# A third K-tile pair by seven products in the up projections, and the retention output from split factors

## The reference

```python
def swiglu(x, w_up, w_down):                      # FFN_HIDDEN = 5632, called twice
    g, u = jnp.split(x @ w_up, 2, axis=-1)
    return (jax.nn.silu(g) * u) @ w_down

def retention(q, k, v):                           # 4 heads, key width 256, value width 512, chunk 128
    ...
        inner = jnp.einsum('bhid,bhjd->bhij', qi, ki) * intra
        o = jnp.einsum('bhij,bhjv->bhiv', inner, vi) + jnp.einsum('bhid,bhdv->bhiv', qi * q_decay, state)
    ...

h = h + 0.5 * rms_norm(swiglu(rms_norm(h, ffn1_pre), ffn1_up, ffn1_down), ffn1_post)
h = h + rms_norm(hybrid_mixer(rms_norm(h, mix_pre), ...), mix_post)
h = h + 0.5 * rms_norm(swiglu(rms_norm(h, ffn2_pre), ffn2_up, ffn2_down), ffn2_post)
```

## Time and profile before

| | |
|---|---|
| median of 3 runs | 2403.52 us |
| the profiled execution: its time | 2403.92 us |
| its span in the trace | 2402.1 us |
| granted TensorE clock, mean | 0.999 |
| PE busy | 2386.3 us, 99%, 10711 instructions |
| PEld busy | 1963.1 us, 82% |
| DVE busy | 1556.8 us, 65%, 1789 instructions |
| ACT busy | 1170.9 us, 49% |
| DMA | 470.98 MB, mean 196 GB/s |

### The profile page before, as it was taken

How to read it: one execution, slowest core, us unless ns; L and a number is a source line. 1 busy time by engine, 2 the same in 40 slices (tenths; PEclk the granted TensorE clock), 3 DMA queues, 4 the chain that set the end, 5 groups by cost and what they waited for, 6 DMA issues and landing times.

```text
span 2402.1 us, 34068 instructions
## 1 busy us (share of the span) xinstructions
PE 2386.3 (99%) x10711; PEld 1963.1 (82%) x10711; DVE 1556.8 (65%) x1789; ACT 1170.9 (49%) x1400; POOL 201.1 (8%) x392
## 2 busy tenths in 40 slices
PE   9999999999999999999999999999999999999998
PEld 7888888888887888887888888888788888888887
DVE  5888888874456555655545545555788888886444
ACT  5555545554445454444534444444655555555443
POOL 1212112110000000000000000000021212111000
PEclk9999999999999999999999999999999999999999
DMA  7665666665656455564666565655566666666564
GB/s 238 211 212 196 226 205 210 218 220 180 205 175 194 152 183 171 162 189 156 200 191 194 192 196 191 194 177 184 176 216 216 210 214 195 226 207 219 191 195 156
DMA packets 265730, 470.98 MB, mean 196 GB/s; under 512 B 21056, under 2 KB 54512, under 8 KB 265296
## 3 DMA queue, kind: packets, MB, share of 16 engines
q1 hardware_dynamic: 252752, 453.04, 58.2%
q0 software_dynamic: 12752, 17.24, 2.3%
q10 hardware_dynamic: 176, 0.07, 0.0%
HBM read 456.64 MB, written 2.10 MB: 191 GB/s over the span
## 4 chain that ended last, share of the span: by engine, by line
PE 98%; DVE 1%; issue 0%; DMA 0%; ACT 0%; POOL 0%; DVEq 0%; ACTq 0%; POOLq 0%
PE acc L673 25%; PE acc L674 24%; PE acc L675 24%; PE acc L766 6%; PE acc L765 6%; PE acc L764 6%; PE bank L764 2%; PE bank L765 2%; PE bank L766 2%; PE bank L694 1%; DVE h L1474 0%; DVE w_lo L1410 0%; PE bank L994 0%; DVE xT_lo L1421 0%; PE bank L934 0%; PE bank L960 0%
## 5 line engine op out<-in xcount | busy, mean ns | idle before, releaser
L1410 DVE TENSOR_TENSOR w_lo<-w_raw,w_hi 128x1024 fp32r<-128x1024 f32 x856 | 1023.9, 1199 | 728.2 <-ACT w_hi L1094 720.8
L1094 ACT ACTIVATE w_hi<-w_raw 128x1024 fp32r<-128x1024 f32 x856 | 888.6, 1040 | 1101.9 <-PE acc L675 845.6
L673 PE MATMUL acc<-w_hi,xT_hi 128*128 128x512 f32 x1664 | 655.3, 394 | 4.1 <-DVE xT_lo L1421 2.4
L675 PE MATMUL acc<-w_hi,xT_lo 128*128 128x512 f32 x1664 | 648.1, 389 | 0.0
L674 PE MATMUL acc<-w_lo,xT_hi 128*128 128x512 f32 x1664 | 647.8, 389 | 0.0
L673 PEld LDWEIGHTS acc<-w_hi,xT_hi 128*128 128x128 f32 x1664 | 312.5, 188 | 71.8 <-DVE xT_lo L1421 3.4
L675 PEld LDWEIGHTS acc<-w_hi,xT_lo 128*128 128x128 f32 x1664 | 312.4, 188 | 65.9
L674 PEld LDWEIGHTS acc<-w_lo,xT_hi 128*128 128x128 f32 x1664 | 312.6, 188 | 64.3 <-issue 1.0
L673 PE MATMUL acc<-w_hi,act_hi 128*128 128x512 f32 x704 | 273.9, 389 | 0.0
L675 PE MATMUL acc<-w_hi,act_lo 128*128 128x512 f32 x704 | 273.9, 389 | 0.0
L674 PE MATMUL acc<-w_lo,act_hi 128*128 128x512 f32 x704 | 273.9, 389 | 0.0
(11 more groups left out here) (202 smaller groups left out, 1862.0 us busy)
## 6 DMA issues: line engine op xcount, KB each, us to landing
w_raw<-in_ffn_up_dram SPq DMA_DIRECT2D x352, 512.0 KB, 4.1
w_raw<-in_ffn_down_dram SPq DMA_DIRECT2D x176, 512.0 KB, 4.1
w_raw<-in_w_gate_dram SPq DMA_DIRECT2D x96, 512.0 KB, 3.7
w_raw<-in_w_in_dram SPq DMA_DIRECT2D x72, 512.0 KB, 3.5
w_raw<-in_w_in_dram SPq DMA_DIRECT2D x128, 256.0 KB, 3.0
w_raw<-in_w_ret_out_dram SPq DMA_DIRECT2D x32, 512.0 KB, 4.7
w_raw<-in_w_out_dram SPq DMA_DIRECT2D x32, 512.0 KB, 4.4
act_raw<-blocks POOLq DMA_DIRECT2D x352, 32.0 KB, 3.7
```

The costliest lines, as they stand in the source:

```text
L673: pe.matmul(pair[m][:, :], xh, wh, start=(first and kk == 0), stop=False)
L675: mm = pe.matmul(pair[m][:, :], xl, wh, start=False, stop=(last and kk == KG - 1))
L1094: act.activation(w_hi[:, s, cols], w_raw[:, s, cols], ACT.Copy).then_inc(w_rounded, 1)
L1410: dve.tensor_tensor(w_lo[:, s, cols], w_raw[:, s, cols], w_hi[:, s, cols].bitcast(f32), ALU.subtract).then_inc(w_split, 1)
```

## The change

`QUADS` has a third pair, so in each of the 20 up strips three K-tile pairs are multiplied by seven products; the order of the groups moves; the third quad uses the first one's place for its sums again. The gate's second token tile is finished before, not behind, the group that DVE splits next. In the heads loop the retention output is made by three fp32r matmuls for each product: ACT and DVE split `innerT` and the value strip into hi and lo parts.

```diff
-QUADS = ((4, 5, 6), (10, 11, 7))
-PLAIN_GATE = ((0, 0), (1, 1), (2, 2), (3, 3), (6, 4), (7, 5))
-PLAIN_UP = ((8, 0), (9, 1), (12, 2), (13, 3), (14, 4), (15, 5))
+QUADS = ((5, 6, 5), (9, 10, 6), (12, 13, 7))
+PLAIN_GATE = ((0, 0), (1, 1), (2, 2), (3, 3), (4, 4))
+PLAIN_UP = ((7, 0), (8, 1), (11, 2), (14, 3), (15, 4))
...
-        T_SLOT = (0, 1)
+        T_SLOT = (1, 0, 1)
...  SP, at the end of an up strip's loads
+                    sp.wait_ge(t_summed, 3 * (quad(f, i, NQUAD - 1) + 1))
+                    sp.sem_inc(slot_summed, 1)
...  PE, heads, n == 25
+            def inner_values(b, block, m, start, stop):
+                cols = slice(block * P, (block + 1) * P)
+                pe.matmul(bank[b][:, :], inner_hi[:, cols], v_hi[:, m, :], start=start, stop=False)
+                pe.matmul(bank[b][:, :], inner_hi[:, cols], v_lo[:, m, :], start=False, stop=False)
+                return pe.matmul(bank[b][:, :], inner_lo[:, cols], v_hi[:, m, :], start=False, stop=stop)
...
+                        pe.wait_ge(inner_split, g + 1)
                         claim("o", 2, g)
-                        pe.matmul(bank[2][:, :], innerT[:, 0:P], gate_sb[:, 0, :], start=True, stop=True).then_inc(filled[2], 1)
+                        inner_values(2, 0, 0, True, True).then_inc(filled[2], 1)
                         claim("o", 3, g)
-                        pe.matmul(bank[3][:, :], innerT[:, P:2 * P], gate_sb[:, 0, :], start=True, stop=False)
-                        pe.matmul(bank[3][:, :], innerT[:, 2 * P:3 * P], gate_sb[:, 1, :], start=False, stop=True).then_inc(filled[3], 1)
+                        inner_values(3, 1, 0, True, False)
+                        inner_values(3, 2, 1, False, True).then_inc(filled[3], 1)
...  ACT, up strip
-                        if n == 10:
+                        if n == 12:
                             wait_filled(act, f"p{f}", 0, i)
                             act.activation(p1_sb[:, :], bank[0][:, :], ACT.Copy).then_inc(read[0], 1)
-                        if n == 13:
+                        if n == 15:
                             wait_strip_read(act, sec, i, 0)
...
-                                    wait_quad_used(act, f, NST - 1, NQUAD - 1)
+                                    wait_quad_used(act, f, NST - 1, 1)
                                 hidden_hi(f, n - 12)
...
+                wait_quad_used(act, f, NST - 1, NQUAD - 1)
                 with act.Fori(0, CH // 2) as i:
...  ACT, heads
+                    if n == 20:
+                        wait_read(act, "inner", 0, g)
+                        act.activation(inner_hi[:, :], innerT[:, :], ACT.Copy).then_inc(inner_rounded, 1)
                     if n == 23:
-                        strip_out(g, n, 2, ACT.Copy)
+                        wait_strip(act, "heads", g, n)
+                        act.wait_ge(rs_ready, MEAN["pre1"] + 1)
+                        for m in range(MT):
+                            last = act.activation(v_hi[:, m, :], acc[pair_of("heads", 2)][m][:, :], ACT.Copy,
+                                                  scale=rs_pre[:, 1, m:m + 1])
+                        last.then_inc(v_rounded, 1)
...  DVE, up strip
-                dve.wait_ge(t_used, quad(f, i, j) + 1)
+                dve.wait_ge(t_used, quad(f, i, j) + (2 if j == 0 else 1))
...
-                        if n == 11:
+                        if n == 13:
                             wait_quad_used(dve, f, i, NQUAD - 1)
...
                             dve.tensor_tensor(u3_sb[:, :], u2_sb[:, :], bank[3][:, :], ALU.add).then_inc(read[3], 1)
-                            wait_filled(dve, f"p{f}", 1, i)
-                            dve.tensor_tensor(u4_sb[:, :], u2_sb[:, :], bank[1][:, :], ALU.add).then_inc(combined, 1)
-                        if n == 12:
                             wait_read(dve, f"p{f}", 3, i)
                             dve.scalar_tensor_tensor(gate_sb[:, 1, :], u3_sb[:, :], to_tile1[:, 0:1], gate[1][:, :],
                                                      ALU.mult, ALU.add).then_inc(acc_read[pair_of(sec, 0)], 1)
+                        if n == 14:
+                            wait_filled(dve, f"p{f}", 1, i)
+                            dve.tensor_tensor(u4_sb[:, :], u2_sb[:, :], bank[1][:, :], ALU.add).then_inc(combined, 1)
                             dve.tensor_tensor(u5_sb[:, :], u3_sb[:, :], bank[1][:, :], ALU.add).then_inc(read[1], 1)
...  DVE, heads
+                    if n == 21:
+                        dve.wait_ge(inner_rounded, g + 1)
+                        dve.tensor_tensor(inner_lo[:, :], innerT[:, :], inner_hi[:, :].bitcast(f32), ALU.subtract).then_inc(inner_split, 1)
+                    if n == 23:
+                        dve.wait_ge(v_rounded, g + 1)
+                        for m in range(MT):
+                            last = dve.scalar_tensor_tensor(v_lo[:, m, :], acc[pair_of("heads", 2)][m][:, :], rs_pre[:, 1, m:m + 1],
+                                                            v_hi[:, m, :].bitcast(f32), ALU.mult, ALU.subtract)
+                        last.then_inc(acc_read[pair_of("heads", 2)], 1)
```

More of the change, by code:

```diff
@@ L169, in hybrid_trunk @@
         hid_sb = sb("hid_sb", [P, MT, STRIP], f32)
+        v_hi = sb("v_hi", [P, MT, STRIP], f32r, at=tmp_at)
+        v_lo = sb("v_lo", [P, MT, STRIP], f32r, at=tmp_at + 4 * MT * STRIP)
         junk = sb("junk", [P, D], f32, at=tmp_at)
@@ L247, in hybrid_trunk @@
         o_junk = sb("o_junk", [P, STRIP], f32, at=s_at)
+        q_at = place["at"]
         qT = sb("qT", [P, 2, SEQ], f32)
+        inner_hi = sb("inner_hi", [P, 3 * P], f32r, at=q_at)
         winT = sb("winT", [P, 2, SEQ], f32)
@@ L251, in hybrid_trunk @@
         rkT = sb("rkT", [P, 2, SEQ], f32)
+        inner_at = place["at"]
         innerT = sb("innerT", [P, 3 * P], f32)
+        inner_lo = sb("inner_lo", [P, 3 * P], f32r, at=inner_at)
         decay = sb("decay", [P, 2 * P], f32)
@@ L304, in hybrid_trunk @@
         k_now_ready = sem("k_now_ready")
+        v_rounded = sem("v_rounded")
+        inner_rounded = sem("inner_rounded")
+        inner_split = sem("inner_split")
         dve_step = sem("dve_step")
```

## The result

| | before | changed |
|---|---|---|
| median, four runs of each | 2403.52 us | 2388.89 us |
| lowest to highest | 2403.48 to 2403.59 | 2388.06 to 2389.58 |
| the profiled execution: time, span | 2403.92, 2402.1 us | 2389.05, 2387.2 us |

The ratio is 0.9939, 95% interval 0.9923 to 0.9955: 14.6 us less. Forecast were 2386.0 us and a range of 2384.3 to 2393.0. The median lies inside that range, but above the 2384.5 to 2388 that the forecast itself gave 0.62; it is in the stretch of rival 1.

A forecast was written before the change was run, and what follows sets the result against it. PE was taken to bound the kernel (98% of the chain). -13.6 - 2.1 - 2.2 + 0.4 = -17.5 from the profiled 2403.92 us gives 2386.4, and 2386.0 us for the median; range 2384.3 to 2393.

The forecast's parts named there:

- rival 1: Gain smaller: small wait moves elsewhere, fp32r beside transposes no faster, last strips lose up to 1 us each; 2387 to 2392, chance 0.16.
- The bound: Whole kernel: PE makes up 98% of the chain, so time goes only where PE does less or waits less.
- part 1: Third quad in each of 20 up strips: three matmuls fewer a strip, 60 x 0.2267 us, -13.6 us.
- The wait for `t_lo`: Up strips: PE's 18 waits for the last `t_lo` of a quad go, 0.12 us each, -2.1 us.
- DVE's dates: Up strips: DVE, 94% busy, still finishes each operand before PE wants it; cost 0.
- The room behind the third quad: Up strips: the third quad's second `t_lo` ends at T = 32.8, 1.9 us before PE needs it.
- The last strip: Last up strip of each block, with two hidden tiles more on DVE: cost 0, up to 1 us in each of two blocks.
- Part 3: Heads loop, retention output: nine fp32r steps (2.04 us) for six float32 records (2.58), four heads, -2.2 us.
- Part 4: Token sums: two more transposes for each block, 4 x 0.11 us, +0.4 us.
- The sum: Whole kernel: all terms together, -17.5 us against the profiled execution's 2403.92 us.
- rival 2: Up strips: loads between quads come late and PE stalls; with 1.6 us late each, 2412 us; chance 0.10.
- rival 3: Up strips: DVE a little behind, each strip loses 0.3 to 0.5 us; 2392 to 2397 us, chance 0.12.

The follow-up runs named there:

- e3: The kernel before, still two quads, with only the first quad one group later (groups 5 and 6 in place of 4 and 5): 2402.11 us.
- e6: The changed kernel with the split of group 14 made twice in each up strip, one DVE instruction more: 2389.24 us.
- e7: The changed kernel with the split of group 14 made three times in each up strip, two DVE instructions more: 2407.05 us.
- e4: The changed kernel with the first hidden tile rounded (ACT, n = 10) and split (DVE, n = 11) earlier in the last strip: 2386.67 us.
- e9: The changed kernel unaltered, timed once more on the same chip as e10: 2388.71 us.
- e10: The kernel of e4 (changed kernel, first hidden tile earlier) timed once more on the same chip as e9: 2386.78 us.
- e1: The kernel before with only the heads loop changed, retention output from split factors: 2401.42 us.
- e8: The changed kernel with the load of group 13 held until group 11 is split, 2.9 us later: 2435.1 us.
- e5: The changed kernel with the gate's second tile finished behind the split of group 2 (n = 14): 2404.59 us.

## Why the prediction was right, and where it missed

- **The bound, and part 1.** PE's step held: 183 steps a strip, period 41.48 as forecast, -13.6 us. By the 216 ns that the Trainium skill gives ("TensorE: Matmul & The Clock Gate", Back-to-back issue gap) the period would be 39.5 us, an estimate from that figure; no run here shows it, the step was 0.2267 us.
- **The wait for `t_lo`.** Forecast -2.1, measured -1.7. It is gone after, and e3 shows it alone. The mechanism was right and the size was not: the 0.12 us came from one pair of strips in the first block and was taken for all 18 waits, while in the second block it is 0.07. (By 0.12 the term would have been -2.16, and its end with all twenty strips -2.4, not -2.2.)
- **DVE's dates.** Laid along PE's time, they were met within 0.4 us: the first list begins at T = 6.55, the third quad's sum at 25.2 (forecast 25.1), its second `t_lo` ends at 32.9 (forecast 32.8), the gate's tile at 39.8 (39.4). In the timeline of DVE, for a strip that begins at 182.25:

```profile
188.80 1.18 DVE L1437 TENSOR_TENSOR w_lo<-w_raw,w_hi 128x1024 fp32r<-128x1024 f32 x1
...
199.70 1.23 DVE L1618 TENSOR_TENSOR t_raw<-w_raw 128x1024 f32<-128x1024 f32 x1 [0.98 <-DMA w_raw<-in_ffn_up_dram]
...
207.48 1.23 DVE L1618 TENSOR_TENSOR t_raw<-w_raw 128x1024 f32<-128x1024 f32 x1
...
213.96 1.22 DVE L1679 TENSOR_TENSOR t_lo<-t_raw,t_hi 128x1024 fp32r<-128x1024 f32 x1
...
221.26 0.75 DVE L1692 SCALAR_TENSOR_TENSOR gate_sb<-u_sb,to_tile,acc 128x512 f32<-128x512 f32 x1
```

  In this strip the wait for the second quad's load was 0.98 us (forecast 0.8), that of the third too small to be marked. The room behind the third quad was put at 1.9; PE's weight load asks a step (0.23) before its matmul, which leaves 1.46 by the trace after, and e6 and e7 bear that out (over 1.25, near 1.5).
- **The last strip: the miss.** "Cost 0, up to 1 us in each of two blocks." I followed DVE's list to group 4, due at T = 52.4, and took the gate's tile and that group for the tight dates. By my own date for the gate's tile, 40.7, the hidden tile's rest behind it ends at 41.9; but I did not ask who waits for it. The first product of the down projection does, at 41.5. Measured 1.0 and 0.8 at the starts, and 0.2 more in each down projection behind them, which goes with the wait (table below); e4, e9 and e10 give back 1.9 to 2.2. The term that was put at 0 is the one that was mis-sized most.
- **Part 3.** Forecast -2.2. The trace has 0.54 for a head, e1 2.3 for all. DVE's two subtracts end at 822.2 in the first head, 2.4 us before PE's first product at 824.62, the room that was forecast.
- **Part 4.** Forecast +0.4. No run tested it alone, but the trace after has six of these transposes in each block, 0.109 us apart, where the kernel before had four: +0.44.
- **The sum.** -17.5 plus the 1.8 of the hand-overs is -15.7 against the profiled execution's -14.9. The rest can be found by stages. Distances between starts of PE, us:

| stretch | before | changed | e3 | e4 |
|---|---|---|---|---|
| last transpose of the token sums to the first product of the down projection, block 1 | 433.69 | 426.82 | 432.62 | 425.83 |
| the same, block 2 | 433.30 | 426.64 | 432.64 | 425.82 |
| first product of the first down projection to the first transpose of `k_twice` | 278.85 | 279.08 | 278.86 | 278.85 |
| from there to the first product of `poolT_hi` (the heads) | 418.81 | 416.57 | 418.81 | 416.57 |
| first to last product of the second down projection | 239.13 | 239.30 | 239.13 | 239.13 |

  The hand-overs cost 2.2 us (changed less e4 over the first three rows and the last), not 1.8, and the `t_lo` wait 1.7 (before less e3). Then -13.6 - 1.7 - 2.2 + 0.4 + 2.2 is -14.9, which is what was measured; nothing of size is left open in these traces.
- **The rivals.** Rival 1 is what happened, at its small end. Its 2387 to 2392 took in the median, and of its three causes one happened, the last strips; the wait did not move elsewhere and the fp32r products beside transposes kept their step. Rivals 2 and 3 did not happen: the period is 41.48 us in all 18 distances and no wait for `t_lo` is left. e8 shows that a late load does reach PE as rival 2 had it, and that its price was set too low: a load 2.9 us late cost 2.1 us a strip, not the 1.0 that is left of 2.9 by its room of 1.9. The Trainium skill ("DMA: Bandwidth & Descriptors", Latency and other measured facts) has HBM latency at 0.2 us on average and 2 us at high load. No growth of that kind shows here: the median from issue to landing of these loads went from 4.1 to 4.2 us, and DVE's waits for loads fell from 30.0 us in 20 to 20.4 us in 26, the longest from 2.0 to 1.2 us.

## What to carry to other kernels

Where PE is full, a saving in products is worth its steps only as long as each consumer's date is met: write the second engine's list along PE's time, and check every product's operand at its first use, at the hand-over to the next stage too, where work that was put beside a quiet stretch meets the new one. Here a second engine at 94%, even at 96% in e6, cost next to nothing while it reached a free moment in each period; when a wait took that away (e8), the price was 2.1 us a strip where the distance to one date gave 1.3. And read a small wait in every stage where it occurs before multiplying it: it was 0.12 us in one block and 0.07 in the other. A three-product fp32r split of a float32 matmul whose factors can be split beside PE is worth 0.18 us for each 128 x 512 product here.

## What the runs showed of the hardware

Matmuls of fp32r with 512 columns kept 0.227 us from start to start in every stage, at a granted clock of 1.00 and with the operands in new places too. Only the first one after a wait was followed 0.33 to 0.34 us later (473.61 to 473.94 at the hand-over, 184.03 to 184.37 in e5). A float32 matmul of the same size takes 0.86 us, 3.8 of those steps, so that three fp32r products in its place save a fifth. The name that the profile gives to a wait need not be the cause: in e5 PEld's 20 waits at the strip's start are put down to `w_lo` (20.1 us), PE's at the same place to the gate's tile (11.8), and the tile is what the edit moved.
